# Context tokens loaded behind the first weights, and normalized and transposed inside the projection's first steps

## The chip, the cores and the metric

The kernel runs on one core of a Trainium2 chip. TensorE (PE) multiplies, VectorE (DVE), ScalarE (ACT) and GpSimd (POOL) compute beside it, and SyncE (SP) issues most loads; each engine runs its own list of instructions in order and meets the others only at semaphores. The metric is the device time of one execution in microseconds (us). Less is better.

## The reference, cut to what matters

One layer of a diffusion backbone: 512 latent tokens `x` and 256 context tokens `ctx`, each 1024 wide, all float32.

```python
mod_x = silu(c) @ w_ada + b_ada            # 6 * 1024 numbers: shift, scale, gate, twice
mod_c = silu(c_ctx) @ w_ada + b_ada
hc = rms(ctx, norm_pre_mix) * (1 + csc1) + csh1
kv = hc @ w_in[:, K_OFF:G_OFF]             # the context gives only keys and values
hx = rms(x, norm_pre_mix) * (1 + sc1) + sh1
mix_x = mixer(hx, w_in, states_from(kv))   # retention heads and Fourier groups
x = x + g1 * rms(mix_x @ w_out)
h2 = modulate(rms(x, norm_pre_ffn), sh2, sc2)
x = x + g2 * rms(peer(h2, w_query, keys, u, v))   # 16384 single-neuron experts
```

The change touches the start only: the first 1024 or 2048 columns of `mod_x` and `mod_c`, the two `rms`, and the first 512 columns of `hx @ w_in` and `hc @ w_in` (the keys).

## The kernel before, in words

Every matmul in full precision is made of three with split operands (`split_mm`, L1721): a tensor is rounded to a high half by ACT (`..._hi`) and DVE subtracts to get the low half (`..._lo`). So each operand passes ACT and then DVE before PE can use it.

The start, up to about 43 us, runs like this. SP issues, into one queue, the load of `x` (`xs`, 2 MB), of the context (`cx`, 1 MB), of eight chunks of `w_ada` (1 MB each), and of four units of `w_in` (`raw`, 0.5 MB each), L495 to L499. PE first runs matmuls on a tile of ones (`keep_busy(WARM)`, L1770). Then it multiplies the chunks of `w_ada` with the two conditioning vectors: chunks 0 and 1 unsplit (`ada_chunk`), chunks 2 to 7 split (`ada_split`), the last in two halves. Between the chunks lie the transposes (`transposed(kc)`, L1757): for each of 8 column blocks four 128x128 tiles of `xs` and two of `cx`, into PSUM banks 4 to 7. ACT takes the `x` columns out of PSUM (`take_x`) and DVE the context's (`take_context`, L1079). Before that, ACT and DVE square and sum the rows, ACT takes the root, DVE scales (`scaled`, L1044).

When the products with `w_ada` are whole, ACT and DVE copy them to `mod_rows`, PE turns them into columns, and DVE forms `mod_a` and `mod_b` (`modulation`, L1066). Then come four weight units of the first projection piece. For each column block `kc` DVE modulates `x` and context (`modulated`, L1117), ACT rounds, DVE subtracts (`modulated_rest`, L1125), and PE multiplies 4 row blocks of `x` and 2 of the context with half a weight unit, 18 matmuls per `kc` (L1862 to L1869). It waits at `full_lo` ahead of the `x` rows and ahead of the context rows of each `kc`.

POOL loads the other 32 pieces of `w_ada` (`part_w`, L605), from the moment that all transposes are done (`tr_done`, L604). There are four buffers; two of them lie where `cx` lies. DVE multiplies and adds these pieces (`add_parts`, L1129) between its later work, in a fixed order with `rest_unit`, the low halves of the weight units. The list of DVE after piece 32 goes on with `up_lo` (L1253), which PE needs in `turn()` (L1842), behind weight unit 12; what DVE does after `turn()` feeds the Fourier and retention parts.

The rest of the kernel, from 160 us on, is not touched by the change.

Of the kernel before, what the change touches and what calls it, by code (L numbers as in the profile page):

```python
# [28 lines left out]
P = 128  # L29
# [161 lines left out]
def build(nc, x, ctxt, cols, w_ada, w_in, w_out, w_q, keys, u_t, u_nat, v_nat, rope, fourier, ident_in,  # L191
# [5 lines left out]
    with es:  # L197
# [167 lines left out]
        junk = at("junk", rJ + 4 * K, [D])  # L365
        full2 = at("full2", rI, [KC, N])
# [22 lines left out]
        xt_taken, ct_taken = sem("xt_taken"), sem("ct_taken")  # L389
# [98 lines left out]
        def _(sp):  # L488
# [7 lines left out]
            sp.dma_start(cx[:], ctxt.rearrange("(b p) d -> p b d", p=P)).then_inc(cx_in, 16)  # L496
# [76 lines left out]
        def _(pool):  # L573
# [30 lines left out]
            pool.wait_ge(tr_done, 2 * KC)  # L604
# [39 lines left out]
        def _(act):  # L644
# [9 lines left out]
            def squares(srcs, first):  # L654
                for m, (src, bank) in enumerate(srcs):
                    if first + m:

                        act.wait_ge(sq_done, first + m)
                    act.activation(junk[:], src, ACT.Square, accum_out=ss[:, bank:bank + 1]).then_inc(sq_done, 1)
# [15 lines left out]
            def take_x(kc):  # L675
                act.wait_ge(tr_done, 2 * kc + 1)
                act.activation(xT[:, kc, :], ps[:, 4 + 2 * kc % 4, :], ACT.Copy).then_inc(xt_taken, 1)
# [60 lines left out]
            act.activation(mod_rows[0:4, D:3 * 512], ps[0:4, 2, :], ACT.Copy).then_inc(rows_out, 1)  # L738

            for p in range(n_proj):  # L740
                for j in range(4):
# [6 lines left out]
                    if p == 0:  # L748

                        for kc in range(2 * j, 2 * j + 2):  # L750
                            round_full(xT[:, kc, :], hT_hi[:, kc, :], 2 * kc)
                            round_full(cxT[:, kc, :], cT_hi[:, kc, :], 2 * kc + 1)
# [137 lines left out]
            for m in range(KC):  # L890
                if m in ACT_COLUMNS:
                    act.wait_ge(tr_done, 2 * KC + m + 1)
# [140 lines left out]
        def _(dve):  # L1033
# [10 lines left out]
            def scaled(i, t, first, count):  # L1044
# [3 lines left out]
                                  ALU.add).then_inc(ms_done, 1)  # L1048
                dve.wait_ge(rt_done, i + 1)
# [5 lines left out]

            scaled(0, xs, 0, TB)
            scaled(1, cx, TB, CB)
# [21 lines left out]
            def take_context(kc):  # L1079
                dve.wait_ge(tr_done, 2 * kc + 2)  # L1080
                dve.tensor_copy(cxT[:, kc, :], ps[:, 4 + (2 * kc + 1) % 4, 0:NCTX]).then_inc(ct_taken, 1)

# [15 lines left out]
            take_context(6)  # L1098
            take_context(7)
# [17 lines left out]
            def modulated(kc):  # L1117
                for m, t in ((2 * kc, xT), (2 * kc + 1, cxT)):
                    if kc == 0:
                        dve.wait_ge(xt_taken, KC)  # L1120
                        dve.wait_ge(ct_taken, KC)
                    dve.tensor_scalar(t[:, kc, :], t[:, kc, :], mod_a[:, kc, m % 2:m % 2 + 1],
                                      mod_b[:, kc, m % 2:m % 2 + 1], ALU.mult, ALU.add).then_inc(full_done, 1)

            def modulated_rest(kc):  # L1125
                for m, t, hi, lo in ((2 * kc, xT, hT_hi, hT_lo), (2 * kc + 1, cxT, cT_hi, cT_lo)):
# [1149 lines left out]
```

## Time and profile before

| | |
|---|---|
| three runs | 1508.92, 1510.31, 1511.13 us, median 1510.31 |
| profiled execution | 1510.31 us, of which the span of its instructions 1508.5 us |
| PE busy | 1491.7 us, 99% of the span |
| DVE, ACT, POOL busy | 1253.2, 589.1, 425.9 us |
| granted TensorE clock | 1.00 over the span |
| first product with `w_ada` | starts at 14.36 us |
| first matmul of the projection | starts at 42.86 us |

The three runs differ by 2.2 us, or 0.15%. A busy PE is not a PE at its peak, but where it is busy without a gap nothing else sets the time. So the stretches to look at are those in which PE waits, and the work that stands on PE itself.

### The profile page before, as it was taken

What the parts mean: (1) busy time and instruction counts of PE and PEld (TensorE: products, weight loads), DVE (VectorE), ACT (ScalarE), POOL (GpSimd) and SP (SyncE); (2) the same over time, 40 slices, a digit from 0 to 9 for tenths busy, and PEclk for the clock granted to TensorE, in tenths of its full rate; (3) what the DMA queues carried; (4) which work ended last, traced back from release to release, by engine and by line L of the source; (5) the groups of instructions that cost most, each with busy time, mean ns of one, the idle gap of its engine ahead of it and who ended that gap; (6) DMA issues with size and microseconds to landing.
All of it is one profiled execution on the core that took longest, in us unless ns stands there. A gap on an engine that the chain in (4) does not pass through costs nothing.

```text
span 1508.5 us, 21819 instructions
## 1 busy us (share of the span) xinstructions
PE 1491.7 (99%) x8129; PEld 1314.1 (87%) x8129; DVE 1253.2 (83%) x2378; ACT 589.1 (39%) x877; POOL 425.9 (28%) x365
## 2 busy tenths in 40 slices
PE   9999999999999999999999999999999999999998
PEld 4788888788999999999999999988888888888886
DVE  6888748766899999899999955697888888888886
ACT  6433134622333334344454443343333333333333
POOL 1020000000468886433222201221322222222210
PEclk9999999999999999999999999999999999999999
DMA  9675113134359896789999999999999999999983
GB/s 389 219 290 177 56 57 98 56 84 154 119 181 306 282 312 219 274 325 364 371 372 364 373 330 353 369 406 372 367 357 372 365 387 395 377 361 368 364 320 132
DMA packets 148439, 431.41 MB, mean 286 GB/s; under 512 B 13328, under 2 KB 46352, under 8 KB 145424
## 3 DMA queue, kind: packets, MB, share of 16 engines
q1 hardware_dynamic: 73152, 203.91, 37.0%
q0 software_dynamic: 41472, 151.01, 27.3%
q10 hardware_dynamic: 33744, 75.64, 13.3%
q8 instruction: 32, 0.52, 0.1%
q14 instruction: 39, 0.32, 0.1%
HBM read 375.98 MB, written 54.53 MB: 285 GB/s over the span
## 4 chain that ended last, share of the span: by engine, by line
PE 81%; DVE 15%; DMA 2%; issue 1%; ACT 1%; POOL 0%; SPq 0%; ACTq 0%; DVEq 0%
PE ps L1723 24%; PE ps L1725 24%; PE ps L1724 24%; PE ps L2134 3%; DVE rows L1520 2%; DVE ps L1552 1%; DVE ps L1556 1%; DVE picks L1558 1%; PE ps L2074 1%; DMA ada_w<-w_ada 1%; DMA grp_w<-w_dram 1%; DVE tv L1486 1%; DVE tv L1489 1%; DVE ti L1490 1%; DVE ti L1487 1%
## 5 line engine op out<-in xcount | busy, mean ns | idle before, releaser
L1723 PE MATMUL ps<-hT_hi,ws_hi 128*128 128x384 f32 (+1 forms) x976 | 341.1, 349 | 2.4 <-POOL ws_lo L617 1.4
L1725 PE MATMUL ps<-hT_hi,ws_lo 128*128 128x384 f32 (+1 forms) x976 | 335.3, 344 | 0.0
L1724 PE MATMUL ps<-hT_lo,ws_hi 128*128 128x384 f32 (+1 forms) x976 | 335.1, 343 | 0.0
L1723 PE MATMUL ps<-vs_hi,coef_hi 128*128 128x512 f32 x768 | 299.0, 389 | 3.2 <-DVE coef_lo L1682 3.2
L1724 PE MATMUL ps<-vs_lo,coef_hi 128*128 128x512 f32 x768 | 298.8, 389 | 0.0
L1725 PE MATMUL ps<-vs_hi,coef_lo 128*128 128x512 f32 x768 | 298.8, 389 | 0.0
L973 ACT ACTIVATE vs_hi<-blk_raw 128x1024 fp32r<-128x1024 f32 x128 | 135.6, 1060 | 285.9 <-PE ps L1725 283.5
L625 POOL DMA_INDIRECT rows<-u_nat,ids x128 | 143.3, 1120 | 301.9 <-DVE sp_act L1520 293.7
L625 POOL DMA_INDIRECT rows<-v_nat,ids x128 | 127.2, 994 | 332.2 <-DVE ps L1640 298.0
L1679 DVE TENSOR_TENSOR vs_lo<-blk_raw,vs_hi 128x1024 fp32r<-128x1024 f32 x128 | 156.6, 1223 | 66.7 <-ACT vs_hi L973 65.5
L919 ACT ACTIVATE ws_hi<-blk_raw 128x1024 fp32r<-128x1024 f32 x102 | 108.1, 1060 | 244.0 <-PE ps L1725 234.5
L1723 PEld LDWEIGHTS ps<-hT_hi,ws_hi 128*128 128x128 f32 x976 | 183.4, 188 | 9.5 <-issue 2.2
L1725 PEld LDWEIGHTS ps<-hT_hi,ws_lo 128*128 128x128 f32 x976 | 183.2, 188 | 6.3
L1724 PEld LDWEIGHTS ps<-hT_lo,ws_hi 128*128 128x128 f32 x976 | 183.5, 188 | 5.5
L1723 PEld LDWEIGHTS ps<-vs_hi,coef_hi 128*128 128x128 f32 x768 | 144.1, 188 | 33.9 <-issue 3.5
L1725 PEld LDWEIGHTS ps<-vs_hi,coef_lo 128*128 128x128 f32 x768 | 144.1, 188 | 29.9
L1724 PEld LDWEIGHTS ps<-vs_lo,coef_hi 128*128 128x128 f32 x768 | 144.1, 188 | 29.8
L1640 DVE SCALAR_TENSOR_TENSOR ps<-rows,sp_coef,ps 128x1024 f32<-128x1024 f32 x127 | 162.9, 1283 | 1.9
L1520 DVE CUSTOM_DVE_ANT_0 rows<-rows,ps 128x1024 f32<-128x1024 f32 x128 | 153.6, 1214 | 0.9
L1652 DVE TENSOR_TENSOR ws_lo<-blk_raw,ws_hi 128x1024 fp32r<-128x1024 f32 x74 | 90.7, 1225 | 56.2 <-ACT ws_hi L919 52.9
L617 POOL TENSOR_TENSOR ws_lo<-blk_raw,ws_hi 128x1024 fp32r<-128x1024 f32 x28 | 69.3, 2474 | 237.9 <-ACT ws_hi L919 237.6
L975 ACT ACTIVATE coef_hi<-coef 128x384 fp32r<-128x384 f32 x128 | 66.0, 515 | 35.0 <-DVE coef L1672 35.0
(329 smaller groups left out, 2266.2 us busy)
## 6 DMA issues: line engine op xcount, KB each, us to landing
blk_raw<-u_t SPq DMA_DIRECT2D x128, 512.0 KB
blk_raw<-v_nat SPq DMA_DIRECT2D x128, 512.0 KB
g_dram<-g_buf ACTq DMA_DIRECT2D x128, 192.0 KB
w_dram<-w_stage SPq DMA_DIRECT2D x48, 512.0 KB
grp_g<-g_dram ACTq DMA_DIRECT2D x15, 1536.0 KB
grp_w<-w_dram ACTq DMA_DIRECT2D x15, 1536.0 KB
part_w<-w_ada POOLq DMA_DIRECT2D x32, 512.0 KB, 6.2
raw<-w_in SPq DMA_DIRECT2D x20, 512.0 KB, 6.0
```

Of the source, the lines that this page charges most:

```text
L617: pool.tensor_tensor(us_lo[u_slot(b)][:], blk_raw[b % U_RING][:], us_hi[u_slot(b)][:].bitcast(F32), ALU.subtract).then_inc(u_lo, 1)
L625: pool.indirect_dma_start(rows[row_slot(k)][:], None, u_nat if k < PICKS else v_nat, bass.IndirectOffsetOnAxis(ids[:, k % PICKS:k % PICKS ...
L919: act.activation(us_hi[u_slot(b)][:], blk_raw[b % U_RING][:], ACT.Copy).then_inc(u_hi, 1)
L973: act.activation(vs_hi[b % V_RING][:], blk_raw[b % U_RING][:], ACT.Copy).then_inc(v_hi, 1)
L975: act.activation(coef_hi[:, b % V_RING, :], coef[:, b % 2, :], ACT.Copy).then_inc(coef_r, 1)
L1520: dve.tensor_tensor_reduce(rows[row_slot(k)][:], rows[row_slot(k)][:], wide, 1.0, 0.0, ALU.mult, ALU.add, sp_act[:, k:k + 1]).then_inc(row ...
L1640: ins = dve.scalar_tensor_tensor(wide, rows[row_slot(g)][:], sp_coef[:, k:k + 1], wide, ALU.mult, ALU.add)
L1652: dve.tensor_tensor(us_lo[u_slot(b)][:], blk_raw[b % U_RING][:], us_hi[u_slot(b)][:].bitcast(F32), ALU.subtract).then_inc(u_lo, 1)
L1679: dve.tensor_tensor(vs_lo[p][:], blk_raw[b % U_RING][:], vs_hi[p][:].bitcast(F32), ALU.subtract).then_inc(v_lo, 1)
L1723: pe.matmul(o, lh, rh, start=start, stop=False, skip_group_check=True)
L1724: pe.matmul(o, lh, rl, start=False, stop=False, skip_group_check=True)
L1725: return pe.matmul(o, ll, rh, start=False, stop=stop, skip_group_check=True)
```

## The change

The load of `cx` is issued behind the eight chunks of `w_ada` and the first weight unit. ACT squares it after it has copied `mod_rows`, into a junk tile of its own, and takes the root behind the first rounding. DVE scales `cx` behind the first low half of `x`. PE transposes the context's column blocks inside the first projection piece: blocks 0 to 3 ahead of the fourth row block of the first `kc`, 4 and 5 inside `kc` 1, 6 and 7 inside `kc` 3, into PSUM banks 6 and 7, two blocks to a bank. DVE no longer copies them out of PSUM: it modulates straight from there. POOL's loads of the remaining pieces of `w_ada` now wait for the last of the context's transposes (`ctr_done`).

```diff
             sp.dma_start(xs[:], ...).then_inc(x_in, 16)
-            sp.dma_start(cx[:], ...).then_inc(cx_in, 16)
             for kc in range(KC):
                 sp.dma_start(ada_w[kc][:], ...).then_inc(ada_in[kc], 16)
-            for n in range(n_units):
+            load_unit(0)
+            sp.dma_start(cx[:], ...).then_inc(cx_in, 16)
+            for n in range(1, n_units):
                 if n == 8:
+                    sp.wait_ge(tr_done, KC)
                     sp.dma_start(tab_raw[:], fourier).then_inc(dft_in, 16)
...
-            pool.wait_ge(tr_done, 2 * KC)
+            pool.wait_ge(ctr_done, KC)
             for u in range(parts):
...
-            act.wait_ge(cx_in, 16)
-            squares([(cx[:, tb, :], TB + tb) for tb in range(CB)], 2)
-            act.wait_ge(ms_done, 4)
-            act.activation(rs[:, TB:TB + CB], ss[:, TB:TB + CB], ACT.Sqrt).then_inc(rt_done, 1)
...
             act.activation(mod_rows[0:4, D:3 * 512], ps[0:4, 2, :], ACT.Copy).then_inc(rows_out, 1)
+            act.wait_ge(cx_in, 16)
+            squares([(cx[:, tb, :], TB + tb) for tb in range(CB)], 2)
...
                             round_full(xT[:, kc, :], hT_hi[:, kc, :], 2 * kc)
+                            if kc == 0:
+                                act.wait_ge(ms_done, 4)
+                                act.activation(rs[:, TB:TB + CB], ...).then_inc(rt_done, 1)
...
-            for kc in range(4):
-                take_context(kc)
-            rest_ada(2)
-            rest_ada(3)
-            take_context(4)
-            take_context(5)
-            for kc in range(4, KC - 1):
+            for kc in range(2, KC - 1):
                 rest_ada(kc)
...
-            for j in range(4):
-                modulated(2 * j)
-                modulated_rest(2 * j)
-                modulated(2 * j + 1)
-                modulated_rest(2 * j + 1)
-                if j < 3:
-                    rest_unit(j + 1)
+            for kc in range(KC):
+                modulated(kc, 0)
+                if kc == 0:
+                    mean_of(1, TB, CB)
+                    modulated_rest(0, 0)
+                    scaled(1, cx, TB, CB)
+                modulated(kc, 1)
+                if kc:
+                    modulated_rest(kc, 0)
+                modulated_rest(kc, 1)
+                if kc in (1, 3, 5):
+                    rest_unit(kc // 2 + 1)
...
+            def context_transposed(kc):
+                if kc == 0:
+                    pe.wait_ge(xn_done, TB + CB)
+                if kc >= 4:
+                    pe.wait_ge(full_done, 4 * (kc // 2 - 1))
+                for cb in range(CB):
+                    col = kc % 2 * NCTX + cb * P
+                    last = pe.transpose(ps[:, 6 + kc // 2 % 2, col:col + P], cx[:, cb, kc * P:(kc + 1) * P], ident[:])
+                last.then_inc(ctr_done, 1)
...
                         for r, (th, tl, tb, bank) in enumerate(rows_of):
                             if r in (0, TB):
                                 pe.wait_ge(full_lo, 2 * kc + 1 + r // TB)
+                            if kc == 0 and r == TB - 1:
+                                for first in range(4):
+                                    context_transposed(first)
+                            if r == TB and kc in (1, 3):
+                                context_transposed(kc + 3)
+                                context_transposed(kc + 4)
```

The list of VectorE at the start of the first projection piece, before; `modulated` is L1122, `modulated_rest` L1115, `rest_unit` L1106:

```order
L1074 SCALAR_TENSOR_TENSOR mod_a<-mod_b,colp 128x16
L1122 TENSOR_SCALAR xT<-xT,mod_a,mod_b 128x512
L1122 TENSOR_SCALAR cxT<-cxT,mod_a,mod_b 128x256
L1115 TENSOR_TENSOR hT_lo<-xT,hT_hi 128x512
L1115 TENSOR_TENSOR cT_lo<-cxT,cT_hi 128x256
L1122 TENSOR_SCALAR xT<-xT,mod_a,mod_b 128x512
L1122 TENSOR_SCALAR cxT<-cxT,mod_a,mod_b 128x256
L1115 TENSOR_TENSOR hT_lo<-xT,hT_hi 128x512
```

The same place on VectorE after the change; there `modulated` is L1121, `modulated_rest` L1109, the mean L1051, reciprocal and scaling L1056 and L1059:

```order
L1080 SCALAR_TENSOR_TENSOR mod_a<-mod_b,colp 128x16
L1121 TENSOR_SCALAR xT<-xT,mod_a,mod_b 128x512
L1051 TENSOR_SCALAR ss<-ss 128x2
L1109 TENSOR_TENSOR hT_lo<-xT,hT_hi 128x512
L1056 RECIPROCAL rs<-rs 128x2
L1059 TENSOR_SCALAR cx<-cx,rs 128x1024 x2
L1121 TENSOR_SCALAR cxT<-ps,mod_a,mod_b 128x256
L1109 TENSOR_TENSOR cT_lo<-cxT,cT_hi 128x256
L1121 TENSOR_SCALAR xT<-xT,mod_a,mod_b 128x512
L1121 TENSOR_SCALAR cxT<-ps,mod_a,mod_b 128x256
L1109 TENSOR_TENSOR hT_lo<-xT,hT_hi 128x512
```

Mean, reciprocal and scaling of the context now stand between the first and the second column block of `x`, and the source of the context's modulation is PSUM.

The list of TensorE in the first `kc` of the first weight unit, after the change; it is the same before, less the row of `cx` (there L1766, in the stretch of `w_ada`, two transposes behind every four of `xs`):

```order
L1729 MATMUL ps<-ws_hi_116,hT_lo 128x512
L1777 MATMUL ps<-ident,cx 128x128 x8
L1727 MATMUL ps<-ws_hi_116,hT_hi 128x512
L1728 MATMUL ps<-ws_lo_120,hT_hi 128x512
L1729 MATMUL ps<-ws_hi_116,hT_lo 128x512
L1727 MATMUL ps<-ws_hi_116,cT_hi 128x512
L1728 MATMUL ps<-ws_lo_120,cT_hi 128x512
```

Eight transposes stand between the third and the fourth row block, three matmuls ahead of the first context rows.

The same list before, around the second chunk of `w_ada`:

```order
L1766 MATMUL ps<-ident,xs 128x128 x4
L1766 MATMUL ps<-ident,cx 128x128 x2
L1736 MATMUL ps<-ada_w_65,csil 4x512 x4
L1766 MATMUL ps<-ident,xs 128x128 x4
L1766 MATMUL ps<-ident,cx 128x128 x2
L1766 MATMUL ps<-ident,xs 128x128 x4
L1766 MATMUL ps<-ident,cx 128x128 x2
L1747 MATMUL ps<-ada_hi_72,csil_r 4x512 x4
```

All the rows of `cx` leave this stretch; nothing else in it moves.

## Rows read from the trace of the kernel before

**Rows 1.** The page: busy time, share of the span, instructions of each engine

```profile
PE 1491.7 (99%) x8129; PEld 1314.1 (87%) x8129; DVE 1253.2 (83%) x2378; ACT 589.1 (39%) x877; POOL 425.9 (28%) x365
```

**Rows 2.** Chain of waits up to 150 us: start, duration, what ran or landed

```profile
1.79 12.44 DMA ada_w<-w_ada
...
37.28 1.02 ACT mod_rows L735
...
39.08 1.13 DVE ws_lo L1106
...
41.36 0.64 ACT hT_hi L673
```

**Rows 3.** TensorE in order of time: start, duration, line, idle before

```profile
1.05 12.88 PE L1730 MATMUL ps<-ones 128*128 128x512 f32 x24 [1.05 <-POOL ones L575]
14.36 3.59 PE L1736 MATMUL ps<-ada_w,csil 128*4 128x512 f32 x8 [0.44 <-DMA ada_w<-w_ada]
...
18.38 0.38 PE L1766 MATMUL ps<-ident,cx 128*128 128x128 f32 x2
18.60 0.60 PE L1766 MATMUL ps<-ident,xs 128*128 128x128 f32 x4
...
42.86 0.48 PE L1723 MATMUL ps<-ws_hi,hT_hi 128*128 128x512 f32 x1 [1.16 <-DVE hT_lo L1115]
...
45.68 0.39 PE L1723 MATMUL ps<-ws_hi,cT_hi 128*128 128x512 f32 x1
```

**Rows 4.** Busy time by stretch, clock, DMA share and GB/s, 10 to 20 us

```profile
10.00:20.00 10.00, 9.56 (x37) 4.08 (x36) 7.33 (x16) 5.53 (x13) 0.00 (x0) 1.00 1.02 430
```

**Rows 5.** ScalarE in order of time, start of the kernel

```profile
12.20 1.04 ACT L659 ACTIVATE junk<-cx 128x1024 f32<-128x1024 f32 x1
...
14.32 0.19 ACT L659 ACTIVATION_READ_ACCUMULATOR junk<-cx 128x1 f32 x1
...
18.58 1.26 ACT L677 ACTIVATE xT<-ps 128x512 f32<-128x512 f32 x2 [2.99 <-PE ps L1766]
...
32.21 2.01 ACT L684 ACTIVATE ada_hi<-ada_w 128x1024 fp32r<-128x1024 f32 x2 [0.40 <-DMA ada_w<-w_ada]
...
38.21 0.59 ACT L738 ACTIVATE mod_rows<-ps 4x512 f32<-4x512 f32 x1
```

**Rows 6.** VectorE in order of time, start of the kernel

```profile
15.82 1.42 DVE L1053 TENSOR_SCALAR cx<-cx,rs 128x1024 f32<-128x1024 f32 x2
18.80 0.42 DVE L1081 COPY cxT<-ps 128x256 f32<-128x256 f32 x1 [1.56 <-PE ps L1766]
...
27.31 8.96 DVE L1085 TENSOR_TENSOR ada_lo<-ada_w,ada_hi 128x2048 fp32r<-128x2048 f32 x5
...
40.78 0.55 DVE L1122 TENSOR_SCALAR xT<-xT,mod_a,mod_b 128x512 f32<-128x512 f32 x1
41.25 0.41 DVE L1122 TENSOR_SCALAR cxT<-cxT,mod_a,mod_b 128x256 f32<-128x256 f32 x1
42.02 0.69 DVE L1115 TENSOR_TENSOR hT_lo<-xT,hT_hi 128x512 fp32r<-128x512 f32 x1 [0.37 <-ACT hT_hi L673]
...
62.62 0.75 DVE L1135 TENSOR_SCALAR part_acc<-part_w,csil 128x1024 f32<-128x1024 f32 x1
```

**Rows 7.** GpSimd's loads in order of time

```profile
31.08 2.35 POOL L609 DMA_DIRECT2D part_w<-w_ada  x4 [27.91 <-PE ps L1766]
```

**Rows 8.** The instructions of tile part_w, 30 to 80 us

```profile
DMA to landing us min/median/max: 4.3/6.3/10.4
```

**Rows 9.** VectorE in order of time, around the turn

```profile
132.61 1.28 DVE L1253 TENSOR_TENSOR up_lo<-ps,up_hi 128x512 fp32r<-128x512 f32 x2
...
137.51 2.48 DVE L1276 TENSOR_TENSOR eo_hi<-low,ps 128x512 fp32r<-128x512 f32 x4 [1.23 <-PE ps L1849]
```

**Rows 10.** TensorE in order of time, the turn's first matmul

```profile
135.45 0.39 PE L1849 MATMUL ps<-up_hi,tab_hi 128*128 128x512 f32 x1
```

**Rows 11.** Who waited for whom, TensorE, 40 to 260 us

```profile
PE ps L1723 <- DVE hT_lo L1115: 1.2, 1, 1.2
```

More of the change, by code:

```diff
@@ L658, in squares @@
                         act.wait_ge(sq_done, first + m)
-                    act.activation(junk[:], src, ACT.Square, accum_out=ss[:, bank:bank + 1]).then_inc(sq_done, 1)
+                    act.activation((junk_c if first else junk)[:], src, ACT.Square,
+                                   accum_out=ss[:, bank:bank + 1]).then_inc(sq_done, 1)
             act.activation(guard[:], csil[:, 0, 2:3], ACT.Sqrt)
@@ L675, in take_x @@
             def take_x(kc):
-                act.wait_ge(tr_done, 2 * kc + 1)
-                act.activation(xT[:, kc, :], ps[:, 4 + 2 * kc % 4, :], ACT.Copy).then_inc(xt_taken, 1)
+                act.wait_ge(tr_done, kc + 1)
+                act.activation(xT[:, kc, :], ps[:, 4 + kc % 4, :], ACT.Copy).then_inc(xt_taken, 1)
             def round_ada(kc, cols=slice(0, 2 * D)):
@@ L1042, in _, with mean_of @@
                                          ss[:, tb:tb + 1]).then_inc(ms_done, 1)
-            def scaled(i, t, first, count):
+            def mean_of(i, first, count):
                 dve.wait_ge(sq_done, 2 * i + 2)
@@ L1048, in scaled @@
                                   ALU.add).then_inc(ms_done, 1)
+            def scaled(i, t, first, count):
                 dve.wait_ge(rt_done, i + 1)
@@ L1115, in rest_of, with context_bank, modulated, modulated_rest @@
                 dve.tensor_tensor(dst, src, hi.bitcast(F32), ALU.subtract).then_inc(full_lo, 1)
[L1117 to L1126, printed above, removed]
-                    rest_of(lo[:, kc, :], t[:, kc, :], hi[:, kc, :], m)
+            def context_bank(kc):
+                return ps[:, 6 + kc // 2 % 2, kc % 2 * NCTX:kc % 2 * NCTX + NCTX]
+            def modulated(kc, context):
+                src, t = ((xT[:, kc, :], xT), (context_bank(kc), cxT))[context]
+                if context:
+                    dve.wait_ge(ctr_done, kc // 2 * 2 + 2)
+                elif kc == 0:
+                    dve.wait_ge(xt_taken, KC)
+                dve.tensor_scalar(t[:, kc, :], src, mod_a[:, kc, context:context + 1],
+                                  mod_b[:, kc, context:context + 1], ALU.mult, ALU.add).then_inc(full_done, 1)
+            def modulated_rest(kc, context):
+                t, hi, lo = ((xT, hT_hi, hT_lo), (cxT, cT_hi, cT_lo))[context]
+                rest_of(lo[:, kc, :], t[:, kc, :], hi[:, kc, :], 2 * kc + context)
             def add_parts(i):
@@ L1757, in transposed @@
             def transposed(kc):
-                for m in (2 * kc, 2 * kc + 1):
-                    if m < 2:
-                        pe.wait_ge(xn_done, (TB, TB + CB)[m])
-                    if m >= 4:
-                        pe.wait_ge(ct_taken if m % 2 else xt_taken, kc - 1)
-                    for tb in range(CB if m % 2 else TB):
-                        src = (cx if m % 2 else xs)[:, tb, kc * P:(kc + 1) * P]
-                        last = pe.transpose(ps[:, 4 + m % 4, tb * P:(tb + 1) * P], src, ident[:])
-                    last.then_inc(tr_done, 1)
+                if kc == 0:
+                    pe.wait_ge(xn_done, TB)
+                if kc >= 4:
+                    pe.wait_ge(xt_taken, kc - 3)
+                for tb in range(TB):
+                    last = pe.transpose(ps[:, 4 + kc % 4, tb * P:(tb + 1) * P], xs[:, tb, kc * P:(kc + 1) * P], ident[:])
+                last.then_inc(tr_done, 1)
+            def context_transposed(kc):
+                if kc == 0:
+                    pe.wait_ge(xn_done, TB + CB)
+                if kc >= 4:
+                    pe.wait_ge(full_done, 4 * (kc // 2 - 1))
[3 more added lines that the diff above has]
+                last.then_inc(ctr_done, 1)
             pe.wait_ge(iotas, 2)
```

18 lines of the change are left out of this document (7 added, 11 removed).

## The prediction

> **What bounds the kernel now.** I read the page first: PE is busy for 99% of the span [rows 1], so a change at the start can win only what PE waits for there, or work that leaves PE. Next the chain of waits over the first 150 us: it begins with the first chunk of `w_ada`, which lands at 1.79 + 12.44 = 14.23 us [rows 2]. That suggests that loads pace the start. PE in order of time says less: PE ends its matmuls on ones at 1.05 + 12.88 = 13.93 us and then waits only 0.44 us for that chunk [rows 3]; behind it PE shows no gap until the products are whole. Then comes a chain of small steps, copies to `mod_rows`, the low half of weight unit 0, first modulation, first rounding [rows 2], ended by the one wait of PE for VectorE, 1.16 us, before 42.86 us [rows 3, 11]. From there to the turn at 135.45 us PE has no other gap of note [rows 10, 11]. So three things can change the end: when the products are whole, what PE does and waits for in the first `kc`, and whether VectorE is in time at the turn.
>
> **The load moved back.** The context is 1.05 MB, and the queue moves 430 GB/s [rows 4]: every chunk of `w_ada` lands 2.4 us earlier, the first at 11.8 us. But PE is on its ones until 13.93 us, so PE starts the first product at about 13.9 instead of 14.36 us: a gain of 0.45 us, not 2.4. The last chunk had held ACT for 0.40 us [rows 5]; that goes too, but PE did not wait for it.
>
> **The transposes taken out of the start.** A pair for the context costs PE 18.60 - 18.38 = 0.22 us [rows 3]; eight pairs are 1.76 us, all in the gapless stretch. They are a gain only if ACT and DVE keep up. ACT's first copy follows PE's first transposes [rows 5], which start 0.5 us earlier, so ACT runs 0.5 to 0.65 us ahead of before, and gains no more where it goes from copy to rounding without a gap; its rounding of the last chunk starts near 31.3 us. DVE loses eight copies of the context, of 0.42 us [rows 6], six of them ahead of the end of its low halves at 27.31 + 8.96 = 36.27 us [rows 6]. Working the three engines through at the durations of before, the last low half is there at 35.0 us and PE wants it at 35.3: a cover of 0.3 us. If that fails, each tenth of lateness costs a tenth. I take the whole gain: products whole 0.45 + 1.76 = 2.2 us earlier. The copies, the low half of unit 0 and the modulation follow unchanged, so DVE begins to modulate at 40.78 - 2.2 = 38.6 us instead of 40.78 [rows 6].
>
> ACT now squares the context in this chain. The two squares take 14.32 + 0.19 - 12.20 = 2.3 us; they start when the copy at 38.21 ends, 38.80 - 2.2 = 36.6 us [rows 5], and end at 38.9 us. The first rounding can start when DVE's first modulation is done, at 41.36 - 2.2 = 39.15 us [rows 2]. So they fit, by 0.25 us. The context itself lands near 33.5 us (one weight unit and itself behind the last chunk, which lands before 30 us), well before.
>
> PE starts the projection at 42.86 - 2.2 = 40.65 us.
>
> **The transposes put into the projection.** The same 16 transposes now cost 1.76 us here, and three changes from one kind of work to another some 0.05 us each: 1.9 us. What PE saved above it pays here. Nothing hides them, because PE has no gap here.
>
> **The waits they bring.** Follow DVE from 38.6 us. First modulation to 39.1, mean to 39.25; the low half of `x` as before, 1.24 to 1.93 us behind the start (42.02 and 0.69 against 40.78) [rows 6], to 40.5; reciprocal 0.2; scaling of `cx` 1.42 us [rows 6], to 42.1 us. PE works off three row blocks at 0.7 each ((45.68 - 42.86) / 4) [rows 3], to 42.8 us, so the scaling is hidden by 0.7 us. Eight transposes to 43.7. The first two blocks are out at 43.35: DVE modulates from PSUM (0.42), ACT rounds (0.4), DVE takes the low half (0.4), three handovers: to 44.7. PE has done its fourth row block at 44.4: **a wait of 0.3 us**. Its two context row blocks last to 46.1. DVE meanwhile modulates block 1 of `x` from 44.6, context, ACT's rounding to 45.8, low half to 46.5: PE **waits 0.45 us** for it. From there DVE needs 5.8 us for two `kc` where PE needs 8.2, so it gains a lead, and before it showed no wait either. Sum of the waits 0.75 us. From both sides: nothing, if DVE and ACT are each a little quicker; and 1.16 + 1.16 = 2.3 us, twice the one wait of this kind in the trace. I take 0.75, since each piece has a row.
>
> Here a row speaks on the new source. The copy of 128x256 out of PSUM takes 0.42 us and the modulation of 128x256 in SBUF 0.41 [rows 6], so I cost the modulation from PSUM at 0.42. The Trainium skill says otherwise in "VectorE: DVE Perf Modes", section "Why PSUM operands drop a tier": a float32 operand in PSUM keeps VectorE at one element a cycle, where SBUF to SBUF with a constant goes twice as fast. By that rule the step costs more by what 256 elements of `x` cost beyond the context's 256 (0.55 - 0.41 = 0.14 us): 0.14 on each of the two steps on PE's path, 0.3 us in all, and the time would be 1511.4. The same 0.14 us is the rival below that names it.
>
> Sum up to unit 1: -0.45 - 1.76 + 1.9 + 0.75 = **+0.45 us**.
>
> **The loads of POOL.** They went out at 31.08 us [rows 7] and had long landed when DVE wanted the first at 62.62 us [rows 6]. Now they wait for the last context transposes, which PE reaches in `kc` 3: 40.65 + 4 x 4.1 + all that is added - 1.4 = 58.5 us. From issue to landing such a load takes 4.3 to 10.4 us, median 6.3 [rows 8]: the first at 63 to 69 us, four together with the table for the Fourier part and weight unit 7 in between. DVE is free for them at 38.6 + 21.8 + 1.8 (mean, reciprocal, scaling) + 2.2 (its waits in the first `kc`) = 64.4 us, 1.8 us later than 62.62. So DVE is late by 1.8 us by its own work, and by up to 6 by the slowest landing. I take 2.3, because the fourth load is wanted only behind three pieces and a weight unit.
>
> This lateness is kept: DVE, POOL and the four buffers run in a ring, and nothing of PE paces them up to the turn. For the weight units it is harmless. At the turn it is not: `up_lo` is done at 132.61 + 1.28 = 133.89 us and PE wants it at 135.45 us [rows 9, 10], a cover of 1.55 us, to which the 0.45 us of PE's own lateness comes: 2.0 us. So 2.3 us of lateness cost 0.3 us. What DVE does behind the turn had waited 1.23 us for PE [rows 9] and moves with it.
>
> **Sum.** +0.45 + 0.3 = +0.75 us, rounded to 0.7. The profiled execution took 1510.31 us (span 1508.5), which is also the median of the runs: **1511.0 us**.
>
> **The rivals.**
>
> A. The start is won and kept, faster. If the loads pace the start as the chain of waits says, and the transposes fall into time that PE would have waited for DVE anyway, both waits in the projection vanish and part of the 1.9 us with them: -2.2 + 1.1 = -1.1 us, 1509.2. For it: the 1.16 us before 42.86. Against it: PE has no gap between 14.36 and the end of the products, nor behind 42.86.
>
> B. The loads of POOL, slower. If the four loads land at the slow end of their range, or the ring runs slower throughout, DVE comes 4.5 to 6 us late to the turn, and PE stands there. It decides from 2.0 us of lateness on and costs each further microsecond in full: +0.45 + 2.5 to 4 = +3 to +4.5 us, about 1514. For it: they are issued 27 us later, beside other loads. Against it: the median landing.
>
> C. The modulation from PSUM at the slower rate: +0.3 us more than the forecast, 1511.4.
>
> D. The squares, or ACT and DVE in the start, miss their cover of 0.25 to 0.3 us: +0.5 us more, 1511.5.
>
> **How the numbers follow.** Forecast 0.45, A 0.17, B 0.15, C 0.13, D 0.10. The likeliest gives 1511.0. For 8 in 10 the range must hold the forecast with its bounds (waits 0 to 2.3, turn 0 to 2), C and D whole, most of A and the lower half of B: 1509.0 to 1513.4. A measurement here tells 0.2% from no change, 3 us. Slower by more than that needs the upper part of B: 0.10. Faster by more than that needs more than the whole 2.2 us of the start and luck beside: 0.04. Within: 0.86.
>
> **What would show it.** After the change: first product with `w_ada` at 13.9 us, no gap of PE up to the end of the products near 36 us, first matmul of the projection near 40.65. PE's waits list has one of about 0.3 us before `cT_hi` and one of about 0.45 before `hT_hi` in the second `kc`. Modulations of the context at 0.42 us (0.55 for C). POOL's loads issued near 58.5 us, DVE's first piece at 64 to 65, `up_lo` at about 135, turn at 136 to 136.5. I am wrong if PE's first matmul of the projection does not come 2 us earlier, or if PE stands at the turn for more than 1 us.

## The result, and the profile after

| | before | after |
|---|---|---|
| runs | 16, median 1510.62 us (1507.99 to 1514.79) | 16, median 1514.31 us (1510.71 to 1519.39) |
| ratio of the times | | 1.0028, 95% interval 1.002 to 1.0036 |
| profiled execution | 1510.31 us, span 1508.5 | 1511.74 us, span 1509.9 |

The change makes the kernel slower by 0.28%, about 4 us. The forecast was 1511.0 us, "within 0.2%" with a chance of 0.86, and a range up to 1513.4: the time lies outside the range, on the side of rival B. The profiled execution of after is one of its quick ones, 2.6 us below the median; "Left open" comes back to that.

TensorE at the start, after the change; columns as in [rows 3]:

```profile
1.05 13.43 PE L1734 MATMUL ps<-ones 128*128 128x512 f32 x24 [1.05 <-POOL ones L578]
14.41 3.60 PE L1740 MATMUL ps<-ada_w,csil 128*4 128x512 f32 x8
...
35.80 0.62 PE L1755 MATMUL ps<-ada_lo,csil_r 128*4 128x512 f32 x2
36.70 1.34 PE L1801 MATMUL ps<-ident,mod_rows 4*128 4x4 f32 x16 [0.28 <-ACT mod_rows L734]
...
41.12 0.47 PE L1727 MATMUL ps<-ws_hi,hT_hi 128*128 128x512 f32 x1 [1.16 <-DVE hT_lo L1109]
...
43.25 1.03 PE L1777 MATMUL ps<-ident,cx 128*128 128x128 f32 x8
...
45.40 0.50 PE L1727 MATMUL ps<-ws_hi,cT_hi 128*128 128x512 f32 x1 [0.41 <-DVE cT_lo L1109]
...
47.25 0.50 PE L1727 MATMUL ps<-ws_hi,hT_hi 128*128 128x512 f32 x1 [0.18 <-DVE hT_lo L1109]
```

The wait of 0.44 us for the first chunk is gone [rows 3], but in this execution the matmuls on ones lasted 0.55 us longer, so the first product starts no earlier. PE is gapless up to the end of the products. The first matmul of the projection starts 1.74 us earlier than before, and the two small waits are there, 0.41 and 0.18 us. The profile counts a wait from the modelled end of the matmul before it. From start to start they cost more: 44.59 to 45.40 us and 46.67 to 47.25 us, 0.81 and 0.58 us where the step is otherwise 0.23, so 0.9 us in all. The same matmul of `kc` 4, behind the last of the transposes, before and after:

```profile
59.28 0.39 PE L1723 MATMUL ps<-ws_hi,hT_hi 128*128 128x512 f32 x1
...
60.58 0.40 PE L1727 MATMUL ps<-ws_hi,hT_hi 128*128 128x512 f32 x1
```

PE is 1.3 us late there, and still 1.3 us when it is ready for the turn.

TensorE at the turn, where [rows 10] had no wait:

```profile
136.53 0.39 PE L1729 MATMUL ps<-ws_hi,hT_lo 128*128 128x512 f32 x1
137.96 0.47 PE L1859 MATMUL ps<-up_hi,tab_hi 128*128 128x512 f32 x1 [1.04 <-DVE up_lo L1257]
```

PE stands there for 1.04 us (1.2 us from start to start), and the turn starts 137.96 - 135.45 = 2.5 us later than before: 1.3 us that PE brings along and 1.2 us of the wait. Up to 885 us that shift hardly changes (2.7 us). VectorE's second operation on the pieces, before:

```profile
63.48 2.67 DVE L1139 SCALAR_TENSOR_TENSOR part_acc<-part_w,csil,part_acc 128x1024 f32<-128x1024 f32 x2
```

VectorE after, from the first `kc` to the turn (compare [rows 6, 9]):

```profile
41.08 1.42 DVE L1059 TENSOR_SCALAR cx<-cx,rs 128x1024 f32<-128x1024 f32 x2
43.89 0.54 DVE L1121 TENSOR_SCALAR cxT<-ps,mod_a,mod_b 128x256 f32<-128x256 f32 x1 [1.39 <-PE ps L1777]
44.92 0.42 DVE L1109 TENSOR_TENSOR cT_lo<-cxT,cT_hi 128x256 fp32r<-128x256 f32 x1 [0.48 <-ACT cT_hi L672]
...
64.92 0.75 DVE L1134 TENSOR_SCALAR part_acc<-part_w,csil 128x1024 f32<-128x1024 f32 x1
68.52 1.28 DVE L1138 SCALAR_TENSOR_TENSOR part_acc<-part_w,csil,part_acc 128x1024 f32<-128x1024 f32 x1 [2.85 <-DMA part_w<-w_ada]
...
133.06 1.28 DVE L1138 SCALAR_TENSOR_TENSOR part_acc<-part_w,csil,part_acc 128x1024 f32<-128x1024 f32 x1 [0.55 <-DMA part_w<-w_ada]
134.26 2.36 DVE L1100 TENSOR_TENSOR ws_lo<-raw,ws_hi 128x1024 fp32r<-128x1024 f32 x2
136.53 1.28 DVE L1257 TENSOR_TENSOR up_lo<-ps,up_hi 128x512 fp32r<-128x512 f32 x2
```

Three things are to be seen. The modulation from PSUM takes 0.54 us, where 0.42 was forecast. DVE starts its first piece of `w_ada` 2.3 us later than before, and then stands 2.85 us for the second piece, where before it went on at once. And `up_lo` starts at 136.53 instead of 132.61 us, 3.9 us late; it stands behind the low halves of two weight units (2.36 us) that nobody wants before the turn. POOL's loads, for [rows 7]:

```profile
59.67 2.58 POOL L612 DMA_DIRECT2D part_w<-w_ada  x4 [56.50 <-PE ps L1777]
```

The chain of waits of after, between the first pieces and the turn (start, duration, what), shows what paces DVE there:

```profile
115.39 6.30 DMA part_w<-w_ada
...
127.02 6.02 DMA part_w<-w_ada
133.18 1.08 issue
134.26 2.36 DVE ws_lo L1100 x2
136.62 1.21 DVE up_lo L1257 x2
137.96 2.10 PE ps L1859 x8
```

A late piece leads to `up_lo` and on to PE. So this is the place to look at; the experiments ask how much of the time it is, and what makes it vary.

### The profile page after: what moved, and what is told of

Its sections match the earlier page's. It is cut to its first block, busy times and chain, and to the rows that moved or that the text cites. A ratio compares the mean times of both kernels' runs of the same rounds, so it can differ in the third digit from the quotient of the medians.

```text
span 1509.9 us, 21812 instructions
## 1 busy us (share of the span) xinstructions
PE 1493.1 (99%) x8129; PEld 1314.0 (87%) x8129; DVE 1251.4 (83%) x2370; ACT 588.9 (39%) x877; POOL 426.3 (28%) x365
## 3 DMA queue, kind: packets, MB, share of 16 engines
q10 hardware_dynamic: 33744, 75.64, 13.3%
## 4 chain that ended last, share of the span: by engine, by line
PE 77%; DVE 16%; DMA 3%; issue 2%; ACT 1%; POOL 0%; ACTq 0%; DVEq 0%; POOLq 0%
PE ps L1727 23%; PE ps L1729 22%; PE ps L1728 22%; PE ps L2150 3%; DMA part_w<-w_ada 3%; DVE rows L1524 2%; DVE ps L1556 1%; DVE ps L1560 1%; DVE picks L1562 1%; PE ps L2090 1%; PE ps L1734 1%; DVE part_acc L1138 1%; DVE tv L1490 1%; DVE tv L1493 1%; DVE ti L1494 1%
```

## The experiments

Theory T (turn): the time is lost where PE waits for `up_lo`. Rival S (start): it is lost in the first `kc`, by the waits and PE's transposes. Rival L (loads): POOL's late start alone makes DVE late. Theory K (clock): a gap of PE also brings a fall of the granted clock behind it. The recorded expectations use other names: theory A (v1, v2) and T (v9) are T here, theory B is S with its cost in the clock, theories 1 and G are K. In a3_after to a5_after, T and S name two places where the clock could fall, the turn and the start of the last stage near 980 us.

Some numbers below are means over all executions of a kernel beside the granted clock of each. The clock of an execution is on record to 0.001 only, so what is split off by it is rough. A fit of all ten kernels' times against that clock, with a level for each kernel and one slope, gives 1.24 us per 0.001 of clock; "at full clock" is a kernel's level relative to before (115 executions, mean 1510.21 us, mean clock 0.9991).

**b_before**, the kernel before against itself, and **a_after**, after once more:

> The kernel before, run as a kernel of its own, so that the granted clock of each of its executions can be read. Theory 1 (the change makes PE lose granted clock in some executions): here nearly all executions have a clock of 1.000, and their times lie within 1508 to 1512 us. Theory 2 (losses of clock come with the chip and the hour, not with the change): the same share of executions as after the change, some 10 of 16, lies at 0.996 to 0.999, and the time goes with it.

> The kernel after, unchanged. Executions with a clock of 1.000 at before + 1 to + 2 us (the profiled one had + 1.4), those below at + 4 to + 8. Theory 1: a clock below 1.000 in half of them or more here, and not in the kernel before beside it. Theory 2: the same in both.

b_before: 1510.66 us, ratio 1.0006 (0.9997 to 1.0015). a_after: 1514.72 us, ratio 1.0027 (1.0018 to 1.0037). The slowdown repeats. In the profile of a_after the ones ended 1.1 us sooner, so the first product came 1.1 us earlier than before, and still the turn was 1.7 us late:

```profile
1.05 12.30 PE L1734 MATMUL ps<-ones 128*128 128x512 f32 x24 [1.05 <-POOL ones L578]
...
137.23 0.47 PE L1859 MATMUL ps<-up_hi,tab_hi 128*128 128x512 f32 x1 [1.44 <-DVE up_lo L1257]
```

Most of what the start wins does not reach the turn: `up_lo` is ready only 0.7 us sooner, and the wait for it grows (1.44 against 1.04 us). 7 of the 12 executions of a_after had a mean granted clock of 0.998 or less, against 2 of 12 of b_before. That is what theory 1 of the expectation says; the prediction had no term for it.

**v1_parts_early**: after, with three of POOL's four first loads as early as before. One `part_w` buffer moves out of the place of `cx` into free space, and the order of the ring changes, so that only its fourth buffer still lies there. The junk tile of the context's squares moves too, away from a buffer that is now loaded early.

```diff
-        part_w = [at(..., (rJ + 8 * K, rJ + 12 * K, rI + 8 * K, rI + 12 * K)[i], [D]) ...]
+        part_w = [at(..., (rS + 19 * K, rI + 8 * K, rI + 12 * K, rJ + 12 * K)[i], [D]) ...]
-            pool.wait_ge(ctr_done, KC)
+            pool.wait_ge(tr_done, KC)
             for u in range(parts):
+                if u == PART_RING - 1:
+                    pool.wait_ge(ctr_done, KC)
```

> The kernel after, but the later pieces of w_ada have other buffers (one in free space, two where nothing lies at that time), so that three of the first four are loaded once the transposes of x are done, as before the change, and only the fourth waits for the context's transposes. This takes away what makes VectorE late to the turn. Wait of PE at the turn: 0 instead of 1.04 us. Theory A (the lateness at the turn, its wait and what follows are the cost): before + 0.4 to + 1.0 us at full clock, and if the wait at the turn is what costs clock, nearly all executions at 1.000, median before + 1. Theory B (the first steps of the projection, transposes between matmuls and the waits there, cost the clock): clock still below 1.000 in half of the executions, median before + 2.5 to + 3.

1510.89 us, ratio 1.0006 (0.9997 to 1.0016): most of the loss is gone by the times. The profile agrees less. DVE starts on the pieces 2.1 us late and goes through them without the 2.85 us:

```profile
64.70 0.74 DVE L1136 TENSOR_SCALAR part_acc<-part_w,csil 128x1024 f32<-128x1024 f32 x1
65.57 2.67 DVE L1140 SCALAR_TENSOR_TENSOR part_acc<-part_w,csil,part_acc 128x1024 f32<-128x1024 f32 x2
...
136.46 1.28 DVE L1259 TENSOR_TENSOR up_lo<-ps,up_hi 128x512 fp32r<-128x512 f32 x2
```

but `up_lo` is 3.9 us late again, and PE waits 1.2 us for it, where the expectation was no wait. So L holds for the start of the ring and by the times of 12 runs (+0.81 us at full clock, standard error 0.4); in the one execution profiled the ring lost the gain again. Why is open.

**v2_before_parts_late**: the reverse, before with POOL's loads about as late as in after.

```diff
-            pool.wait_ge(tr_done, 2 * KC)
+            pool.wait_ge(split_used, 2)
```

> The kernel before, with one line changed: GpSimd's loads of the later pieces of w_ada wait for the second weight unit to be used (about 59.2 us) instead of for the transposes (31 us). VectorE is then late to the turn as after the change. Theory A: a wait of PE at the turn of 0.5 to 1.5 us, and before + 0.5 to + 1.5 us at full clock; if that wait costs clock, a share of executions below 1.000 as after the change, and a median of before + 2 to + 4. Theory B: the wait at the turn, but all executions at 1.000 and a median of before + 0.5 to + 1.5.

POOL issues at 59.77 us, and the time is 1511.54 us, ratio 1.0016 (1.0005 to 1.0026). PE:

```profile
136.66 0.47 PE L1849 MATMUL ps<-up_hi,tab_hi 128*128 128x512 f32 x1 [1.05 <-DVE up_lo L1253]
```

Without any of the other edits, the late loads bring `up_lo` 2.6 us late, a wait of 1.05 us and a shift of 1.3 us from there on. L is shown as a part of the cause, between a half and two thirds: by means this kernel lies 1.9 us above before and after 3.7; at full clock it stands at +1.95 us (standard error 0.4), after at +2.96 (0.25).

**v3_reorder**: after, with the four `x` row blocks of both first `kc` ahead of the context rows of both (on PE, and so in the lists of ACT and DVE).

```diff
+FIRST_STEPS = [(0, 0), (1, 0), (0, 1), (1, 1)]
...
-                        for r, (th, tl, tb, bank) in enumerate(rows_of):
+                    if s == 0:
+                        turns.sort(key=lambda t: t[1] >= TB)
```

> The kernel after, with the first weight unit in another order on the three engines: PE multiplies the x rows of both column blocks before the context rows of either; ACT and DVE follow. This takes the two small waits in the unit (0.41 and 0.18 us) away and saves VectorE about 2 us of idling. Expected: no wait there, VectorE 2 us less late to the turn, its wait 1.0 -> 0; shift against before at 600 us from +2.6 to about +0.9. Theory G: the share of executions at 0.998 or less as before the change, median before + 0.5 to + 1.5. Theory that only the transposes in the projection matter (a mix of transposes and matmuls): median still before + 3.

1512.12 us, ratio 1.0007 (0.9997 to 1.0017). The waits of 0.41 and 0.18 us are gone from PE's list of waits, but at the turn PE waits longer (in all, times, longest):

```profile
PE ps L1877 <- DVE up_lo L1275: 2.3, 1, 2.3
```

Without the wait PE would be 0.3 us late at the turn instead of 1.3, so what S names can be won, about 1 us, and did not get past the turn in this execution. The expectation, no wait at the turn, missed: `up_lo` is 4.1 us late. At full clock the kernel stands at +1.08 us (0.42) against +2.96 of after, which this profile does not explain.

**v5_fill_turn**: after, with two matmuls on ones (four instructions on the array) ahead of the wait at the turn, so that PE has no gap there.

```diff
                 pe.wait_ge(dft_r, 1)
+                pe.wait_ge(proj_taken, 16)
+                for _ in range(2):
+                    pe.matmul(ps[:, 5, :], ones[:], ones[:, 0:1].broadcast_to([P, 512]), start=True, stop=True)
                 pe.wait_ge(f_rest, 2)
```

> The kernel after, with two matmuls on a tile of ones ahead of PE's wait at the turn, about 1.7 us of work into a free bank. The wait at the turn is covered, and costs at most some tenths more than before. Theory G with the turn as the gap: the share of executions at 0.998 or less falls from half to that of the kernel before (about one in eight), median before + 2.0 to + 2.8, against + 4 for the kernel after. If the falls come from elsewhere (first unit, or anywhere): the share stays at half and the median at before + 4 to + 5.

> The kernel after once more, for more executions with their clocks, and for a second or third profile; one that comes with a clock of 0.998 or less shows where the clock fell. Theory G (a gap of PE of one to two microseconds can be followed by 3.4 us at half clock, as in the profile of the kernel before run again, where a gap of 1.95 us at 977 us was): the fall stands within 2 us behind the new wait at the turn (136 to 142 us), or behind the small gaps of the first weight unit (41 to 50 us). Theory R (falls of clock come anywhere): it stands elsewhere. Time: before + 4 us, full-clock executions before + 2.

v5: 1513.71 us, ratio 1.0022 (1.0013 to 1.0031); a2_after beside it 1513.44 us, 1.0022 (1.0012 to 1.0031). No gain. PE has no wait at the turn, and the matmuls on ones stand in its place:

```profile
136.45 1.88 PE L1857 MATMUL ps<-ones 128*128 128x512 f32 x4
138.25 0.50 PE L1862 MATMUL ps<-up_hi,tab_hi 128*128 128x512 f32 x1
```

Here `up_lo` was 4.3 us late, and the 1.88 us just covered the wait that this makes; where the wait would have been 1.0 to 1.1 us, as in three of the six profiles of after, they would cost 0.8 us more than the wait, by estimate. At full clock the kernel stands at +3.72 us (0.42), 0.8 above after, a difference of less than two standard errors, and its mean clock is 0.9994 against 0.9985. If both are taken as they stand, what the clock gave back went into the filling. The share at 0.998 or less fell as theory G expected (2 of 11), the median did not.

**a3_after, a4_after, a5_after**: after, profiled three more times, to catch where the clock falls.

> The kernel after, one profiled execution more. If its clock is 0.998 or less, the trace shows where the falls are. Theory T (the gap at the turn): behind 137 us. Theory S (the wait at the start of the last stage, for the first weights read back, which two kernels so far showed with a fall behind it): at 980 to 990 us. In both the fall should come within 3 us behind a gap of PE.

> The same as a3_after, another execution, with the same expectations of both theories.

> The same as a3_after, another execution, with the same expectations of both theories.

1513.75, 1512.19 and 1514.41 us, with waits at the turn of 2.5, 1.1 and 1.9 us. a4_after has no fall but the one that all 17 profiles have in their last microseconds, a3_after has one at 984 to 988 us (a2_after has one, too, at 980 to 984 us), and a5_after has one right behind the turn:

```profile
138.73 0.47 PE L1859 MATMUL ps<-up_hi,tab_hi 128*128 128x512 f32 x1 [1.91 <-DVE up_lo L1257]
...
139.50 0.45 PE L1859 MATMUL ps<-up_lo,tab_hi 128*128 128x512 f32 x1
139.74 0.63 PE L1859 MATMUL ps<-up_hi,tab_hi 128*128 128x512 f32 x1
140.17 0.63 PE L1859 MATMUL ps<-up_lo,tab_hi 128*128 128x512 f32 x1
...
142.73 0.57 PE L1727 MATMUL ps<-ws_hi,hT_hi 128*128 128x512 f32 x1
143.14 0.39 PE L1728 MATMUL ps<-ws_lo,hT_hi 128*128 128x512 f32 x1
```

Its stretches of 3 us, with the granted clock as the third number from the end:

```profile
135.00:138.00 3.00, 1.82 (x9) 1.16 (x7) 3.00 (x5) 0.79 (x1) 0.00 (x0) 1.00 0.26 32
138.00:141.00 3.00, 2.27 (x7) 1.85 (x8) 2.69 (x13) 0.00 (x0) 0.00 (x0) 0.78 0.88 304
141.00:144.00 3.00, 3.00 (x10) 2.37 (x9) 2.31 (x4) 2.99 (x11) 0.00 (x0) 0.65 0.05 20
144.00:147.00 3.00, 3.00 (x14) 2.47 (x14) 3.00 (x6) 0.62 (x1) 0.00 (x0) 1.00 0.02 5
```

From 139.7 to 143 us the matmuls start every 0.43 us instead of every 0.23: half clock. Eight starts lie 0.2 us further apart each, 1.6 us; against before the shift goes from 3.3 us at the turn to 4.9 us behind it. K is seen once at this place: in one profile of six of after, and in one of the ten profiles of all kernels that have a wait of 0.9 us or more at the turn (the longest, 2.54 us in a3_after, had none behind it).

**v9_up_lo_first**: after, with the two low halves that stand ahead of `up_lo` on DVE moved behind it. Nothing else changes; this shortens the wait and leaves the late loads, the start and the transposes.

```diff
-                    if p < 4 or j:
+                    if (p < 4 or j) and 4 * p + j not in (14, 15):
                         rest_unit(4 * p + j)
...
                                           ALU.subtract).then_inc(f_rest, 1)
+                    rest_unit(14)
+                    rest_unit(15)
```

> The kernel after, with one edit on VectorE: the low halves of weight units 14 and 15 (1.13 us each, wanted by PE 5 and 11 us later) come behind up_lo instead of ahead of it, so that up_lo is ready 2.3 us earlier. Nothing else moves. Theory T (VectorE's lateness at the turn is the larger part of the loss): wait at the turn 1.0 to 2.5 us -> 0 to 0.5, shift against before behind the turn +1.0 to +1.3 us instead of +2.6, mean clock nearer 0.9992 than 0.9984, median before + 1 to + 1.8. If the loss comes from elsewhere, the wait goes and the median stays at before + 3.5 or more.

1510.50 us, ratio 1.0000 (0.9991 to 1.0010), beside 1509.99 us of before. In its profile:

```profile
136.99 0.47 PE L1861 MATMUL ps<-up_hi,tab_hi 128*128 128x512 f32 x1 [0.19 <-DVE up_lo L1257]
```

This is the run that decides. By the medians the whole slowdown goes with the wait at the turn, though `up_lo` still starts 2.9 us later than before (135.55 us). By means: after lies 3.7 us above before, v9 0.45 us. Of these 3.3 us, 2.1 stand at full clock (2.96 against 0.87, standard error of the difference about 0.5), and 1.2 go with the clock (0.9994 against 0.9985 at 1.24 us per 0.001). In the profiled execution PE still comes to the turn 1.2 us late on its own and starts it 1.5 us late. T holds; what is left for S is about 1 us (0.87 at full clock, standard error 0.4).

**v4_all**, a version that was meant to be faster than both: v3 and v1 together, ACT scales `cx` in place of DVE, and 10 instead of 12 matmuls on ones (`WARM`), since the chunk is there earlier. **v4_again** repeats it; **v6_all_warm12** has 12 again; **v10_all_up** adds the edit of v9.

```diff
-WARM = 12
+WARM = 10
...
+                                act.wait_ge(rs_done, 2)
+                                for cb in range(CB):
+                                    act.activation(cx[:, cb, :], cx[:, cb, :], ACT.Copy,
+                                                   scale=rs[:, TB + cb:TB + cb + 1]).then_inc(xn_done, 1)
```

> The candidate: v3, and the later pieces of w_ada loaded early as in v1, the context scaled by ScalarE, which is idle there, instead of by VectorE (1.4 us off VectorE), and two matmuls fewer on the tile of ones at the start, since the first chunk of w_ada now lands 2.4 us earlier (PE starts 1.7 us earlier). Expected: no wait at the turn, shift against before at 600 us of -0.5 to -1.5 us, median before - 1.5 to 0. If the start is paced by ACT and DVE instead, the 1.7 us are lost and the median is before + 0.5.

> The candidate v4 once more beside v6 and v10, to see whether it is faster than before: before - 1.0 to - 2.0 us, ratio 0.9990 to 0.9994.

> The candidate v4 with the full twelve matmuls on the tile of ones at the start. Theory W (the earlier first chunk can only be used when PE is free for it; with twelve matmuls it is not): PE starts the first product at 13.3 to 14.4 us instead of 12.1, and the median is 1.3 to 2.2 us above v4, so before - 0.4 to + 0.6. Rival: ACT and VectorE pace the start, then it is equal to v4, before - 1.5.

> The candidate v4 together with the edit of v9. v4 has no wait at the turn in its profile; if some executions had one, this takes it away too. Expected: before - 2.0 to - 1.0, equal to v4 within 0.7 us.

v4_all: 1508.31 us, ratio 0.9992 (0.9983 to 1.0001); v4_again 1508.65 us, 0.9989 (0.9980 to 0.9998); v6 1509.68 us, 0.9998 (0.9989 to 1.0007); v10 1509.01 us, 0.9992 (0.9983 to 1.0002). PE in v4_all:

```profile
1.05 10.44 PE L1759 MATMUL ps<-ones 128*128 128x512 f32 x20 [1.05 <-POOL ones L585]
12.08 3.59 PE L1765 MATMUL ps<-ada_w,csil 128*4 128x512 f32 x8 [0.59 <-DMA ada_w<-w_ada]
...
38.79 0.47 PE L1752 MATMUL ps<-ws_hi,hT_hi 128*128 128x512 f32 x1 [1.16 <-DVE hT_lo L1125]
...
133.40 0.47 PE L1884 MATMUL ps<-up_hi,tab_hi 128*128 128x512 f32 x1
```

The first product starts 2.3 us earlier than before, the turn 2.1 us earlier and without a wait. The repeat, v4_again, does not look the same: its first product starts at 12.88 us, and the wait at the turn is back:

```profile
135.31 0.47 PE L1884 MATMUL ps<-up_hi,tab_hi 128*128 128x512 f32 x1 [0.92 <-DVE up_lo L1282]
```

In this execution the turn is only 0.1 us early: the candidate, too, can lose its gain there. By the times v4 is 0.1% faster than before; the interval of one of its two measurements touches 1, so this is a gain of 1.3 us at full clock with a standard error of 0.3, not a large one. v6 tells what the ones are worth: with 12 the start is only 0.3 us early, and 0.9 us of the gain are gone (-0.43 against -1.34 at full clock, standard error of the difference 0.5). v10 has no wait at the turn in its profile, with `up_lo` at 129.66 us, and stands at -1.84 us at full clock (0.4); its median adds nothing to v4 that can be told. Its mean clock was 0.9985 with 5 of 12 executions at 0.998 or less, as low as that of after, without a wait at the turn.

## Why the prediction was wrong

**The load moved back.** Said: first product at 13.9 us, a gain of 0.45. Measured: 14.41 us here, 13.3 us in a_after. The reasoning held (PE is bound by its ones, not by the chunk, which had landed), but the ones themselves took 12.1 to 13.6 us from execution to execution, more than the term.

**The transposes taken out of the start, and the squares.** Held. No gap up to the end of the products; the squares of ACT end before the first rounding:

```profile
36.95 1.04 ACT L662 ACTIVATE junk_c<-cx 128x1024 f32<-128x1024 f32 x1
...
39.08 0.19 ACT L662 ACTIVATION_READ_ACCUMULATOR junk_c<-cx 128x1 f32 x1
39.62 0.63 ACT L672 ACTIVATE hT_hi<-xT 128x512 fp32r<-128x512 f32 x1 [0.35 <-DVE xT L1121]
```

Rival D did not come. The projection began 1.74 us earlier, 2.2 less the 0.45 that the ones took.

**The waits in the first `kc`.** Said 0.75 us in two pieces, 0.3 and 0.45; listed 0.41 and 0.18, which from start to start cost 0.9 us. The sum of +0.45 us holds all sixteen transposes; the last four stand in `kc` 3, and behind them PE is 1.3 us late in this execution. Of the 0.85 us too much, 0.5 are the first step; most of the rest are these waits and the first matmul behind each, which takes 0.33 us to the next start instead of 0.23. The transposes with their changes cost 1.8 us (said 1.9, with 0.05 us a change for which no row of before stood; measured about 0.09). The rate of the modulation from PSUM was wrong in the sum and right in rival C: 0.54 us against 0.42. By the section "Why PSUM operands drop a tier" of the Trainium skill ("VectorE: DVE Perf Modes") a float32 operand in PSUM takes the slower rate; the trace agrees, 0.54 us from PSUM against 0.41 in SBUF [rows 6]. The row on which I leaned, the copy of 0.42 us from PSUM, was one of another operation. A low half takes 0.69 us for 512 columns and 0.42 for 256, or 1.05 ns a column; a modulation in SBUF takes 0.55 and 0.41, or 0.55 ns a column and 0.27 us beside them. 0.27 us and 256 columns at 1.05 ns make 0.54 us: by this estimate the modulation took over the slower rate and kept its own fixed part. On PE this cost little, since the wait for the context was still 0.41; on DVE eight modulations of 0.12 us more are 1.0 us, and DVE is the engine that comes late at the turn.

**The loads of POOL.** This is the step that failed. It said that DVE would come 2.3 us late to the turn, against a cover of 1.55 + 0.45 us, and that PE would lose 0.3 us there. The formula for the turn was right: it starts about 1.5 us less late than `up_lo`. The lateness was mis-sized. Six profiles of after, us later than before:

| | second piece on DVE | `up_lo` | PE, ready for the turn | turn | wait of PE |
|---|---|---|---|---|---|
| after | 5.0 | 3.9 | 1.3 | 2.5 | 1.0 |
| a_after | 1.3 | 3.2 | 0.2 | 1.8 | 1.4 |
| a2_after | 1.5 | 2.7 | 0.0 | 1.2 | 1.1 |
| a3_after | 3.8 | 4.2 | 0.1 | 2.8 | 2.5 |
| a4_after | 3.2 | 3.8 | 1.2 | 2.4 | 1.1 |
| a5_after | 5.1 | 4.7 | 1.2 | 3.3 | 1.9 |

In the mean `up_lo` was 3.7 us late (forecast 2.3), PE brought 0.7 us along (forecast 0.45) and lost 1.7 us at the turn from start to start (forecast 0.3). PE stood for over 1 us in each, one of the prediction's own signs of being wrong.

Two parts of the step failed. One is the start of the ring: in after the first four loads are issued together from 59.67 us on, and the piece for DVE's second operation was there only at 68.5 us, 8.8 us later, where the forecast had used the median landing of 6.3 us [rows 8]. The other is the sentence that the lateness is kept. In a_after and a2_after DVE is only 1.3 and 1.5 us late at the second piece and 3.2 and 2.7 us at the turn; in after it is 5.0 and then 3.9. So the ring sets a lateness of its own. Between 60 and 137 us DVE waits 10.8 us for pieces in a_after and 8.3 in before. Which loads collide there no run takes apart. The late loads alone, in before, make `up_lo` 2.6 us late (v2).

**Rival B** named this mechanism and the point from which it decides (2.0 us); the direction is its own. Its price, +3 to +4.5 us, about 1514, fits the median in part by luck. It asked for DVE 4.5 to 6 us late, and only one profile of six reaches that; the turn itself is 1.2 to 3.3 us late, not 3 to 4.5. By means, of the 3.7 us of after, 3.0 stand at full clock, and 0.75 go with its lower clock (0.9985 against 0.9991), which B did not have. Its chance of 0.15 was too low all the same: the step that it rests on had the widest bounds of the whole sum (DVE late by 1.8 to 6 us), and the forecast took a value near the lower one.

**What no step had.** The granted clock. In a5_after the wait of 1.91 us at the turn was followed by 3.4 us at half clock, 1.6 us more. Over all executions 18 of 39 of after had a mean clock of 0.998 or less, 21 of 115 of before, 2 of 12 with the wait shortened (v9) and 2 of 11 with it filled (v5). That looks like K, but it is not shown that the turn is the place. v3, v4_all and v10 had 5 of 11, 4 of 11 and 5 of 12, two of them without a wait at the turn in their profiles. And the four profiles that have a mean clock of 0.998 (b_before, a3_after, v4_again, v5) all have their fall between 980 and 989 us; a5_after, with the fall at the turn, has 0.999. So a lower clock belongs to some executions of after more often than of before, and where most of it is lost is open.

**Left open.** What sets DVE's lateness between the first pieces and the turn (v1, with early loads, goes from 2.1 to 3.9 us); why v1 and v3 were quicker by their times than the shift of their profile says; and how far the waits behind 970 us give back what was lost (PE waited 3.16 us there before and 1.74 after, and the shift fell from 2.7 to 1.2 us, 1.4 at the end). The six profiles of after have a mean shift of 2.4 us at 290 us without the fall, the times say 3.0 at full clock: the last half microsecond is not placed. The profiled execution of after, 2.6 us below its median, has no fall but the last one, the shortest of the six waits at the turn, and that return behind 970 us; whether these make up the 2.6 us is not shown.

## What to carry to other kernels

A gain at the start is worth only what the tightest later meeting of two engines lets through: follow the shift of each engine to the next place where one waits for the other. Where an engine runs in a ring with its loads, do not carry its first lateness forward as it is: here 1.3 and 5.0 us at the start of the ring became 3.2 and 3.9 at its end. Give such a term the whole width of its bounds, in the forecast too. When work moves onto an engine off the critical path, look at what stands in its list directly ahead of the result that is wanted: here moving two low halves behind `up_lo` cured nearly all of the loss (3.3 of 3.7 us by means). And a wait of TensorE can cost twice, once by its length and once by the clock behind it, as one profile shows; since that comes in some executions only, compare means over many of them, not two profiles.

## What the hardware showed that was not expected

The granted clock fell to about half behind some waits of TensorE of 1.8 to 4.4 us, in a stream of matmuls that is otherwise nearly without a gap, and not behind others. Before, too, has such a place, near 978 us; here b_before, stretches of 5 us:

```profile
975.00:980.00 5.00, 3.05 (x17) 2.68 (x16) 2.84 (x4) 2.08 (x3) 0.19 (x1) 1.00 1.00 402
980.00:985.00 5.00, 5.00 (x16) 3.98 (x15) 3.51 (x6) 2.42 (x3) 1.01 (x1) 0.66 1.00 360
985.00:990.00 5.00, 5.00 (x23) 4.13 (x22) 5.00 (x10) 2.51 (x4) 2.02 (x2) 1.00 0.96 363
```

The wait ahead of it was 1.95 us; in the profile shown of before it was 3.16 us, and the clock stayed at 1.00 behind it, as it did behind 2.54 us at the turn in a3_after. Five of the 17 profiles have a fall between 980 and 989 us, one has it at the turn. So the length of the wait alone does not decide. The two levels are 2.4 and 1.2 GHz; 128x512 matmuls start every 0.23 us at one and every 0.43 us at the other.

The matmuls on ones at the start, always the same 24 instructions, took from 12.12 us (a2_after) to 13.61 us (v3), with 12.88 in before and 13.43 in after: the time of this start varies by over a microsecond, more than the 0.75 us of the forecast. Before hardly feels it, since its first chunk lands at about 14.2 us; after does.
